# Transposed block inverse, levels two to five: 32x32 transposes on VectorE and a copy on ScalarE in place of TensorE products; a convolution tap moved

## The reference, cut to what matters

```
a   = where(strict, beta[..., :, None] * einsum('bnhid,bnhjd->bnhij', k, k) * decay, 0)
lhs = a + eye(CHUNK)
sol = triangular_solve(lhs, rhs, left_side=True, lower=True, unit_diagonal=True)
vw, kd = sol[..., :DV], sol[..., DV:]
```

## Time and profile before

| | |
|---|---|
| time before, median of 3 runs | 1068.02 us (1067.87 to 1069.43) |
| span of the profiled execution | 1066.9 us |
| time of the profiled execution as a whole | not listed apart; the span is 1.1 us under the median |
| TensorE busy | 1055.8 us, 99% of the span |
| VectorE, ScalarE, GpSimd busy | 738.1, 573.9, 626.9 us |
| the chain that ended last | PE 92% |
| granted TensorE clock | 0.998 |

### The profile page before, as it was taken

One profiled execution on the slowest core, in us unless ns is written; L12 is line 12 of the kernel. 1 busy time (PEld: TensorE's weight loads), 2 busy tenths in 40 slices (PEclk: granted clock), 3 DMA queues, 4 the chain that ended last, 5 costly groups with the idle time before them and its releaser, 6 DMA issues.

```text
span 1066.9 us, 22163 instructions
## 1 busy us (share of the span) xinstructions
PE 1055.8 (99%) x8147; PEld 1034.1 (97%) x8147; DVE 738.1 (69%) x1237; ACT 573.9 (54%) x1050; POOL 626.9 (59%) x538
## 2 busy tenths in 40 slices
PE   8999999999999999999999999999999999999998
PEld 6999999999999999999999999999999999999997
DVE  7998997969879698797877766495454444444335
ACT  7855645455555555545645965766444434343632
POOL 1886496584865848658584443636555555555631
PEclk9999999999999999999999999999999999999999
DMA  6223112231122321222221162123332223222302
GB/s 241 100 67 111 65 48 86 80 109 63 39 90 82 99 74 39 90 83 80 93 80 60 43 230 82 33 81 100 96 97 86 80 80 102 94 79 79 117 9 84
DMA packets 32652, 92.09 MB, mean 86 GB/s; under 512 B 4689, under 2 KB 12241, under 8 KB 32593
## 3 DMA queue, kind: packets, MB, share of 16 engines
q1 hardware_dynamic: 32592, 91.29, 26.4%
HBM read 82.76 MB, written 8.52 MB: 86 GB/s over the span
## 4 chain that ended last, share of the span: by engine, by line
PE 92%; POOL 3%; issue 1%; DVE 0%; ACT 0%; POOLq 0%; DVEq 0%; ACTq 0%
PE ps L742 34%; PE ps L1153 14%; PE ps L1101 13%; PE ps L751 7%; PE ps L1185 5%; PE ps L707 3%; PE ps L944 1%; PE ps L997 1%; PE ps L761 1%; POOL in_lo L2574 1%; PE ps L913 1%; PE ps L934 1%; PE ps L1006 1%; POOL o_a L2574 1%; PE ps L971 1%
## 5 line engine op out<-in xcount | busy, mean ns | idle before, releaser
L2574 POOL TENSOR_TENSOR w_lo<-raw,w_hi 128x1024 fp32r<-128x1024 f32 x100 | 241.5, 2416 | 217.3 <-ACT w_hi L1277 107.8
L742 PE MATMUL ps<-in_hi,w_hi 128*128 128x288 f32 x944 | 286.3, 304 | 0.5 <-issue 0.5
L742 PE MATMUL ps<-in_hi,w_lo 128*128 128x288 f32 x944 | 283.8, 301 | 0.0
L742 PE MATMUL ps<-in_lo,w_hi 128*128 128x288 f32 x944 | 281.8, 300 | 0.7 <-POOL in_lo L2574 0.7
L1881 DVE SCALAR_TENSOR_TENSOR ps<-work,ct,ps 128x512 f32<-128x512 f32 x240 | 180.7, 753 | 7.2 <-DVE work L2046 1.6
L742 PEld LDWEIGHTS ps<-in_hi,w_hi 128*128 128x128 f32 x944 | 177.7, 188 | 2.0 <-ACT work L1394 0.7
L742 PEld LDWEIGHTS ps<-in_lo,w_hi 128*128 128x128 f32 x944 | 177.3, 188 | 1.0 <-POOL in_lo L2574 0.9
L742 PEld LDWEIGHTS ps<-in_hi,w_lo 128*128 128x128 f32 x944 | 177.6, 188 | 0.5
L1878 DVE TENSOR_TENSOR o_a<-o_a,ps 128x576 f32<-128x576 f32 (+1 forms) x63 | 42.8, 682 | 107.3 <-PE ps L1153 73.3
L2574 POOL TENSOR_TENSOR w_lo<-t_pair,w_hi 128x1024 fp32r<-128x1024 f32 x18 | 43.6, 2421 | 42.5 <-ACT w_hi L1736 29.7
L1277 ACT CAST w_hi<-raw 128x1024 fp32r<-128x1024 f32 x63 | 65.6, 1043 | 0.0
(11 more groups left out here) (394 smaller groups left out, 2864.5 us busy)
## 6 DMA issues: line engine op xcount, KB each, us to landing
raw<-w_all_in SPq DMA_DIRECT2D x135, 512.0 KB, 3.6
work<-s_in_in SPq DMA_DIRECT2D x8, 512.0 KB, 3.3
s_sample_out<-work SPq DMA_DIRECT2D x8, 512.0 KB, 2.7
xt<-x_t_in SPq DMA_DIRECT2D x4, 576.0 KB, 6.4
xt<-x_t_in SPq DMA_DIRECT2D x2, 1152.0 KB, 7.1
y_out<-o_a SPq DMA_DIRECT2D x14, 144.0 KB, 1.7
halo<-halos_in SPq DMA_DIRECT2D x9, 156.0 KB, 3.5
conf_rows_out<-c_rows SPq DMA_DIRECT2D x8, 135.0 KB, 2.1
```

The source lines that it names most:

```text
L742: t = mm(dense_ps(n, j, h), a[:, w, k], b[:, k, h * HALF:(h + 1) * HALF], start=r == 0, stop=r == PASS_MM // 2 - 1)
L2574: return gp.tensor_tensor(out, a, b, op)
```

## The change

At levels two to five the diagonal blocks of T are at most 32 wide, so the transpose of T is a transposition of each 32x32 block. In place of the U product, VectorE transposes T blockwise (two instructions of 64x256, one for each half of the partitions) into `uc_t`, a float32 area in `dm`, and ScalarE copies it (128x256) into `uc_r`, in its even slots 10, 12, 14 and 16, ahead of the copies of X of that slot. TensorE's T product waits for this copy by a new semaphore `uc_ready`. For the samples the level-two product of line 946 goes too, by a transposition of 64x64; that of level three stays. The U products of levels six to eight stay. One convolution tap of VectorE's slot 8 moves to slot 9, behind the head's work of that slot, in all phases. At the program's end GpSimd's wait on `out_gained` goes; it still waits on `expo`, which ScalarE raises later.

The diff, cut to its core:

```diff
+BLOCKWISE = 5
+DU_PRODUCTS = 4
...
+        uc_t = v["dm"][:, 0:SEQ // 2]
...
                         if l == 2:
                             pe.wait_ge(u0_ready, n)
-                            pe.wait_ge(qk_ready, n)
-                            if n_is(n, 1):
-                                pe.wait_ge(vt_ready, 1)
+                        elif l <= BLOCKWISE + 1:
+                            pe.wait_ge(uc_ready, (BLOCKWISE - 1) * (n - 1) + l - 2)
                         else:
                             pe.wait_ge(ui_ready, LEVELS * n - 9 + l)
...
-                        for c in range(TILES):
-                            if l == STEPS:
-                                r = mm(tile(g(1), c), tile(x_last, c), tile(u_r, c), start=True, stop=True)
-                            elif l == LEVELS:
-                                r = mm(cut(g(1), c)[0:HP], low(x_r, c), low(u_r, c), start=True, stop=True)
-                            else:
-                                r = mm(cut(g(1), c), tile(x_r, c), cut(uc_r, c), start=True, stop=True)
-                        if l <= LEVELS_S:
+                        if l == LEVELS_S:
+                            pe.wait_ge(qk_ready, n)
+                            if n_is(n, 1):
+                                pe.wait_ge(vt_ready, 1)
                             r = mm(g(3)[:, 0:SMP], wide("db", SEQ), v["us"], start=True, stop=True)
-                        r.then_inc(du_ps, 1)
+                            r.then_inc(du_ps, 1)
+                        if l > BLOCKWISE:
+                            for c in range(TILES):
...
+                                    r = mm(cut(g(1), c), tile(x_r, c), cut(uc_r, c), start=True, stop=True)
+                            r.then_inc(du_ps, 1)
...
                         l = (s - 4) // 2
                         if s == 8 and n_is(n, 1):
                             v_tile(n)
+                        if 2 < l <= BLOCKWISE + 1:
+                            act.wait_ge(ui_ready, LEVELS * n - 9 + l)
+                            A(uc_r[:, 0:SEQ // 2], uc_t, ACT.Copy).then_inc(uc_ready, 1)
                         act.wait_ge(x_ps, LEVELS * n - 8 + l)
...
-                    dve.wait_ge(du_ps, LEVELS * n - 8 + l)
-                    if l > 2:
+                    if l <= BLOCKWISE:
+                        dve.wait_ge(t_ready, LEVELS * n - 7 + l)
+                        for i in range(2):
+                            r = ve.transpose(pair2(uc_t, i), quad(t_r, i, i).bitcast(F32))
+                        if l < LEVELS_S:
+                            r = ve.transpose(v["us"][0:SMP], v["hms"][0:SMP])
+                    else:
+                        dve.wait_ge(du_ps, DU_PRODUCTS * (n - 1) + l - BLOCKWISE + 1)
                         dve.wait_ge(ui_ready, LEVELS * n - 9 + l)
...
-                    else:
-                        r = tt(pr2(uc_r), pr2(uc_r).bitcast(F32), pr2(g(1)), ALU.subtract)
-                    if l <= LEVELS_S:
+                    if l == LEVELS_S:
+                        dve.wait_ge(du_ps, DU_PRODUCTS * (n - 1) + 1)
+                        dve.wait_ge(ui_ready, LEVELS * n - 9 + l)
                         r = tt(v["us"][0:SMP], v["us"][0:SMP], g(3)[0:SMP, 0:SMP], ALU.subtract)
...
-            early = {1: 4, 2: 2, 3: 3, 8: 2}
+            early = {1: 4, 2: 2, 3: 3, 8: 1, 9: 1}
...
-            early_1 = {1: 3, 2: 1, 3: 3, 8: 3, 10: 1, 12: 1, 16: 1, 18: 1, 19: 2, 20: 2, 21: 3}
+            early_1 = {1: 3, 2: 1, 3: 3, 8: 2, 9: 1, 10: 1, 12: 1, 16: 1, 18: 1, 19: 2, 20: 2, 21: 3}
...
-            pool.wait_ge(out_gained, len(POOL_BLOCKS))
```

More of the change, by code:

```diff
@@ L349, in build @@
         t_ready, u0_ready, ui_ready = sem("t_ready"), sem("u0_ready"), sem("ui_ready")
+        uc_ready = sem("uc_ready")
         x_ps, x_ready, dt_ps, du_ps = sem("x_ps"), sem("x_ready"), sem("dt_ps"), sem("du_ps")
@@ L518, in build @@
         y_ready_p, out_scaled_p = sem("y_ready_p"), sem("out_scaled_p")
-        out_gained = sem("out_gained")
         c1_ready = sem("c1_ready")
@@ L937, in phase @@
                             r.then_inc(dt_ps, 1)
-                        for c in range(TILES):
-                            if l == STEPS:
-                                r = mm(tile(g(1), c), tile(x_last, c), tile(u_r, c), start=True, stop=True)
-                            elif l == LEVELS:
-                                r = mm(cut(g(1), c)[0:HP], low(x_r, c), low(u_r, c), start=True, stop=True)
-                            else:
-                                r = mm(cut(g(1), c), tile(x_r, c), cut(uc_r, c), start=True, stop=True)
-                        if l <= LEVELS_S:
-                            r = mm(g(3)[:, 0:SMP], wide("db", SEQ), v["us"], start=True, stop=True)
-                        r.then_inc(du_ps, 1)
+                        if l == LEVELS_S:
+                            pe.wait_ge(qk_ready, n)
+                            if n_is(n, 1):
+                                pe.wait_ge(vt_ready, 1)
+                            r = mm(g(3)[:, 0:SMP], wide("db", SEQ), v["us"], start=True, stop=True)
+                            r.then_inc(du_ps, 1)
+                        if l > BLOCKWISE:
+                            for c in range(TILES):
+                                if l == STEPS:
+                                    r = mm(tile(g(1), c), tile(x_last, c), tile(u_r, c), start=True, stop=True)
+                                elif l == LEVELS:
+                                    r = mm(cut(g(1), c)[0:HP], low(x_r, c), low(u_r, c), start=True, stop=True)
+                                else:
+                                    r = mm(cut(g(1), c), tile(x_r, c), cut(uc_r, c), start=True, stop=True)
+                            r.then_inc(du_ps, 1)
                     if s == 22:
@@ L1862, in _ @@
                     A(half_of(o_a[:, j], 1), half_of(o_a[:, j], 1), ACT.Copy,
-                      scale=pcol("post_ffn", j)).then_inc(out_gained, 1)
+                      scale=pcol("post_ffn", j))
                 if i == H:
@@ L2116, in head @@
                         r.then_inc(t_ready, 1)
-                    dve.wait_ge(du_ps, LEVELS * n - 8 + l)
-                    if l > 2:
+                    if l <= BLOCKWISE:
[4 more added lines that the diff above has]
+                            r = ve.transpose(v["us"][0:SMP], v["hms"][0:SMP])
+                    else:
+                        dve.wait_ge(du_ps, DU_PRODUCTS * (n - 1) + l - BLOCKWISE + 1)
                         dve.wait_ge(ui_ready, LEVELS * n - 9 + l)
-                    else:
-                        dve.wait_ge(u0_ready, n)
                     if l == STEPS:
@@ L2159, in head @@
                     stt(o, v["db"], pcol("delta_g", 0), v["zs"], ALU.mult, ALU.mult).then_inc(head_out, 1)
-            early = {1: 4, 2: 2, 3: 3, 8: 2}
-            early_8 = {1: 4, 2: 3, 6: 2, 8: 2}
+            early = {1: 4, 2: 2, 3: 3, 8: 1, 9: 1}
+            early_8 = {1: 4, 2: 3, 6: 2, 8: 1, 9: 1}
             late = {22: 2, 23: 2, 24: 4, 25: 2, 26: 2, 27: 2, 28: 2, 29: 1, 30: 2, 31: 1}
             late_1 = {24: 4, 25: 2, 26: 3, 27: 2, 28: 2, 29: 1, 30: 2, 31: 1}
-            early_1 = {1: 3, 2: 1, 3: 3, 8: 3, 10: 1, 12: 1, 16: 1, 18: 1, 19: 2, 20: 2, 21: 3}
-            early_2 = {1: 4, 2: 1, 3: 3, 8: 3, 10: 1, 12: 1, 16: 1}
+            early_1 = {1: 3, 2: 1, 3: 3, 8: 2, 9: 1, 10: 1, 12: 1, 16: 1, 18: 1, 19: 2, 20: 2, 21: 3}
+            early_2 = {1: 4, 2: 1, 3: 3, 8: 2, 9: 1, 10: 1, 12: 1, 16: 1}
             def convolutions(n, s):
```

1 line of the change is left out of this document (removed).

## The result

| | before | after |
|---|---|---|
| median, both in the same series | 1067.94 us (1067.65 to 1069.43) | 1075.06 us (1074.46 to 1075.63) |
| ratio, 95% interval | | 1.0063 (1.0051 to 1.0075) |
| span of the profiled execution | 1066.9 us | 1073.7 us |
| TensorE busy | 1055.8 us | 1049.2 us |

The changed kernel is 7.1 us slower; the spans differ by 6.8. Part 1 of the page, beside the earlier trace rows: engine, busy us, share of the span, instructions.

What follows compares the result with a forecast made beforehand. TensorE's matmul stream was taken to bound the kernel. Gains of 0.25 us in five heads and 0.9 in the last, against losses of 1.55 in two, made it 1.0 slower: 1069.0 us, range 1063 to 1077.

Steps and rivals of the forecast that it cites:

- forecast case: Transpositions on VectorE of 0.37 to 0.49 us, giving 1066 to 1074 us, centre 1069.0; chance 0.48.
- rival B: VectorE's transpositions in slots 9 to 15 take 0.5 us or more: loss 6 to 18, 1074 to 1086 us; chance 0.22.
- What is removed: TensorE's products of lines 944 and 946: 13.4 and 1.8 us, together 15.2 us, 1.90 for each head.
- The price of a transposition: On VectorE, 0.42 us for 64x256 and 0.21 for 64x64, taken from the nearest rows.
- Level three: Head 4: transpositions, then ScalarE's copies, let the T product start at 4.37, dense work ends at 3.74: wait 0.63 us.
- The copy of U as a link: ScalarE's 128x256 copy, priced 0.41 us, stands in the path between the transpositions and TensorE's T product.
- V: Experiments' theory that VectorE's load makes it late: 0.89 us of transposition pairs per level against the 0.42 update replaced.
- S: The prediction's view, tested later: TensorE waits for the serial chain through ScalarE's copy, 0.42 us per wait before T.
- Level six and seven in heads 3 to 7: Level six: X late by 0.08 us, the copy behind T by 0.29; level seven: wait 0.77.
- Heads 1 and 2: Three more taps between levels three and seven: waits of 3.84 us, 0.37 before; each head loses about 1.55.
- Rival D: The change works as said, but heads 1 and 2 lose nothing because taps find gaps: 1065.4 us; chance 0.09.
- The last head: No new wait up to level five; X of level seven waits for VectorE's layer norm chain; gain 0.9 us.

Runs made afterwards that it cites:

- copy_only: Changed kernel without the two 64x256 transpositions per level, ScalarE's copy kept but reading T directly; 1057.53 us, ratio 0.9897.
- wide: Changed kernel with one 128x512 transposition per level in place of two of 64x256, and two ScalarE copies in place of one; 1070.63 us.
- levels_2_4: Like `levels_3_4`, but transpositions at levels two to four in heads 2 to 7; 1063.79 us, ratio 0.9960 against the kernel before.
- taps_moved: Changed kernel with the three extra convolution taps of heads 1 and 2 moved from slots 10, 12, 16 to slots 1 to 3; 1076.24 us.
- levels_3_4: Kernel before with moved tap, `order2`'s cast and splits, transpositions in the last head and at levels three and four of heads 2 to 7; 1062.06 us.
- order2: Changed kernel, ScalarE's slot-18 cast behind level seven's copy of X, GpSimd's splits of slots 18 and 20 behind the Conformer gate and sum; 1067.27 us.
- order: Changed kernel with ScalarE's slot-18 cast behind level seven's copy of X and GpSimd's slot-18 split behind T minus identity; 1069.33 us.

## Why the prediction was right, and where it failed

The time was 1075.1, inside the range (1063 to 1077) but 6 us above the forecast and 2 above the range of the forecast case (1066 to 1073); slower, to which 0.39 was given. It lies inside only because rival B had widened the range, and B's condition, transpositions of 0.5 us or more, did not hold (0.439): that part is luck. That a product taken out is worth its own pitch (1.89 us for each of heads 3 to 7, counted from the T products to the next dense matmul, for 1.90), and that VectorE had almost no reserve, is what happened. Line by line, span against span (measured: the lengths of the heads):

| | predicted | measured |
|---|---|---|
| heads 3 to 7 | 5 x -0.25 = -1.3 | 5 x +0.74 = +3.7 |
| heads 1 and 2 | 2 x +1.55 = +3.1 | 2 x +2.23 = +4.5 |
| last head | -0.9 | -1.54 |
| sum | +1.0 | +6.6 |

- **What is removed**: right in kind; 32 matmuls of line 953 are left. That free transpositions would not give all 15.2 us was not in the sum; 10.4 is what `copy_only` gives.
- **The price of a transposition**: 0.42 and 0.21 were taken from the nearest rows, 0.439 and 0.237 were measured. The estimate from the Trainium skill (VectorE: DVE Perf Modes, The three transpose paths) had 0.44; the trace, with 0.439, agrees with it. By the prediction's own sensitivity that is 1.3 us of the miss.
- **Level three**: "transpositions, then ScalarE copies, wait 0.63". T came 4.58 us after T of level two (282.12 to 286.70), 4.37 was predicted: 0.1 late where ScalarE's copies end (286.45), and another 0.1 from there to the product (0.25 for 0.14). TensorE lost 0.72 there for 0.63, in two places: 0.41 ahead of T and 0.31 among the dense matmuls of slot 11. T itself was released by ScalarE's last copy, and in heads 1 and 2, where slot 11 runs through, T3 alone waits 0.70 and 0.81; so here the 0.31 lies inside the same wait and adds nothing to it. Those 0.31 stand where the job begins whose weights GpSimd splits; the split ended at 285.17, the matmul began at 285.41. It stands in the same place, in heads 4 to 7, in every kernel with the loop's products of level two out (`copy_only` 0.13 to 0.17, `wide` 0.2, `levels_2_4` 0.27 to 0.29) and in none with them in. That it is the split was read from these rows, not tried.
- **The copy of U as a link**: here the reasoning failed, though the gaps it foretold came. The last link to end before a wait is not the cause when the next wait is set by another chain; without the copy TensorE waits as long one step later. My test ("no gap at level three would be wrong") could not tell V from S.
- **Level six and seven in heads 3 to 7**: X6 0.27, T6 0.44, T7 0.71 against 0.08, 0.29, 0.77. Each pair takes 0.89 and not 0.84, four times; VectorE's lateness adds up over levels.
- **Level eight**: the step that was missing. The prediction followed the cast on ScalarE to the copy of X and stopped. The same cast releases GpSimd's split, behind which T minus identity is queued, for x_last and T8: 0.28 in each of five heads, 1.4 us that no step of the sum held. Moving both took it away.
- **Heads 1 and 2**: 4.2 us of waits from T3 to T7 in each against 3.84, in the direction of the higher price. `taps_moved` shows that the three taps make the difference to the others. Rival D falls. (Its 3.6 us hold 0.25 of gain in each of the two heads; losing nothing would have been 3.1, 1065.9.)
- **The last head**: -1.54 and not -0.9. I let its X7 wait pay 0.5 for the transpositions; but it is 0.93 in `copy_only` too, with no transposition of 64x256 at all, so that TensorE's earlier arrival alone makes it.
- **The tap**: it pays, but 0.15 in each of heads 3 to 7.
- **Rival B** named the right time for a wrong reason. Its warning row, 1209 ns for 128x512 with both operands in SBUF, is a mean of seven of 0.684 and one of 4.88 us, and no transposition was stretched at all.

About 0.15 of the 0.75 in head 4 is in no wait of the table. The starts of the matmuls show where it is: products that follow a wait take longer to the next dense matmul (T6 0.68 for 0.65, T7 0.46 for 0.44, T8 0.50 for 0.43), about 0.1 in all, and the stretch from T8 to the next head is 0.05 longer (41.40 for 41.35).

## What to carry to other kernels

When work goes from a full engine to one that is 70% busy, look at the second one's reserve in the stretch, not over the span: here the 28.1 us of transpositions cost 17.5 us of time (`copy_only`). To find what binds, take out one link of the chain and see whether the waits fall or only move; a releaser's name is the last link, not the cause. Follow an instruction that others wait for (here one weight cast) on every engine that it releases, and convert only the steps behind which the stream has room: in the same order of work two levels gained 2.5 us over none (`levels_3_4`) and four lost 2.7 (`order2`, which has them in head 1 too). The heads differ: against none, four levels still gain 0.2 in each of heads 3 to 7, and lose 1.9 and 1.5 in heads 1 and 2, where VectorE had the least reserve.

## What the runs showed of the hardware

A transposition by 32x32 blocks in fp32 takes 0.439 us for 64x256 and 0.712 for 128x512, and one of 64x64 took 0.237 in the changed kernel. From 64 to 256 columns, both on 64 partitions, that is 1.05 ns for a column ((439 - 237) / 192); carried on to 512 columns it gives 0.71 as an estimate, which is what 128 partitions took, so twice the partitions cost nothing that shows. The one of 64x64 took 0.194 in `wide`; why is open. 52 of the changed kernel's 72 lay within an instruction of GpSimd, and none was stretched: all 64 of 64x256 took 436 to 444 ns, all eight of 64x64 236 to 238.

Other VectorE instructions were stretched. A copy of 128x32 between two tiles in SBUF takes 0.25 us in the kernel before and 2.00 in `order`, where it starts inside GpSimd's pair of splits and ends 0.04 after it, at 306.58. The same copy is as long in each of heads 2 to 7 of `order` (1.99 to 2.01 us), and each ends about 0.04 after a split. VectorE, then GpSimd:

```profile
304.58 2.00 DVE L2205 COPY ct<-tap 128x32 f32 x1
```
```profile
301.82 4.72 POOL L2591 TENSOR_TENSOR w_lo<-raw,w_hi 128x1024 fp32r<-128x1024 f32 x2
```

The instruction with two operands in SBUF that took 4.88 us, in the last head of the kernel before, lies across GpSimd's too, and ends 0.55 us after the last of them. The seven of 0.684 started 0.6 us ahead of GpSimd's next instruction. VectorE, then GpSimd:

```profile
538.64 4.88 DVE L1878 TENSOR_TENSOR work<-work,hc 128x512 f32<-128x512 f32 x1
```
```profile
537.10 2.37 POOL L2574 TENSOR_TENSOR w_lo<-raw,w_hi 128x1024 fp32r<-128x1024 f32 x1
539.43 2.16 POOL L2574 TENSOR_TENSOR work<-work,ct 128x992 f32<-128x992 f32 x1
541.55 1.42 POOL L2574 TENSOR_TENSOR work<-work 128x576 f32<-128x576 f32 x1
```

The Trainium skill (SBUF — State Buffer, Who interferes with whom) says that a VectorE instruction with two SBUF inputs contends with a GpSimd instruction that reads SBUF, that one in a two-port mode, into which copies can go, locks the ports that it shares with GpSimd so that the one that comes second waits it out, and that one with at most one SBUF input outside these modes does not contend. These rows agree, as far as they go: no row shows in which mode the copy ran. The page does not name transpositions; they have one SBUF input, and that none was stretched fits the third case. By that rule rival B's contention would have had no ground.
